# Turning a second softmax unit of five groups by VectorE and DMAs in a dense attention loop

## What is computed

```python
def latent_attention(q_nope, q_rope, k_nope, k_rope, v):
    ...
    def one_block(args):
        qn_b, qr_b = args
        s = (jnp.einsum('bqhd,bkhd->bhqk', qn_b, k_nope)
             + jnp.einsum('bqhr,bkr->bhqk', qr_b, k_rope)).astype(jnp.float32) * scale
        p = jax.nn.softmax(s, axis=-1).astype(v.dtype)
        return jnp.einsum('bhqk,bkhd->bqhd', p, v)
```

## Time and profile before

| | us |
|---|---|
| median of 3 runs | 606.72 (605.74 to 607.55) |
| profiled execution, its time | 606.28 |
| its span | 604.4 |
| TensorE busy | 595.3 (98%) |
| VectorE busy | 446.4 (74%) |
| ScalarE busy | 356.3 (59%) |
| GpSimd busy | 292.4 (48%) |
| hardware DMA queue, share of 16 engines | 56.2% |

### The profile page before, as it was taken

One profiled execution on the slowest core, in us unless ns is written; L12 is line 12 of the kernel. 1 busy time (PEld: TensorE's weight loads), 2 busy tenths in 40 slices (PEclk: granted clock), 3 DMA queues, 4 the chain that ended last, 5 costly groups with the idle time before them and its releaser, 6 DMA issues.

```text
span 604.4 us, 9197 instructions
## 1 busy us (share of the span) xinstructions
PE 595.3 (98%) x3076; PEld 484.0 (80%) x3076; DVE 446.4 (74%) x802; ACT 356.3 (59%) x762; POOL 292.4 (48%) x273
## 2 busy tenths in 40 slices
PE   8999999999999999999999999999999999999996
PEld 7888888788888888888887777777777777888885
DVE  5777663334434439898899788998998988799884
ACT  6644223213333228777787678788788788524563
POOL 4610702515656532536556537677677776510601
PEclk9999999999999999999999999999999999999998
DMA  7587457774776720101015967767768745598042
GB/s 246 190 287 203 155 166 242 230 259 149 245 262 226 224 69 1 36 1 36 2 27 114 242 157 185 190 179 191 192 172 199 203 127 182 177 386 326 1 173 107
DMA packets 72431, 102.11 MB, mean 169 GB/s; under 512 B 10232, under 2 KB 43008, under 8 KB 72384
## 3 DMA queue, kind: packets, MB, share of 16 engines
q1 hardware_dynamic: 72224, 101.25, 56.2%
q10 hardware_dynamic: 160, 0.27, 0.1%
HBM read 60.17 MB, written 31.62 MB: 152 GB/s over the span
## 4 chain that ended last, share of the span: by engine, by line
PE 78%; DMA 8%; DVE 5%; ACT 3%; POOL 2%; SPq 2%; issue 1%; ACTq 0%; DVEq 0%
PE ps L1824 13%; PE ps L1826 13%; PE ps L1825 13%; PE ps L2118 9%; PE ps L2096 7%; PE ps L2026 5%; PE ps L2031 5%; PE ps L1996 3%; PE ps L2046 2%; DMA lat_scratch<-lat_b 2%; PE ps L2006 2%; DMA lat<-lat_scratch 2%; PE ps L1983 2%; PE ps L1982 2%; PE ps L2007 2%; DMA ukv_raw<-w_ukv 1%
## 5 line engine op out<-in xcount | busy, mean ns | idle before, releaser
L1674 DVE TENSOR_TENSOR pT_lo<-ps,pT_hi 128x512 fp32r<-128x512 f32 x102 | 69.3, 684 | 21.5 <-ACT pT_hi L1237 20.3
L1824 PE MATMUL ps<-hT_hi,w_hi 128*128 128x512 f32 x208 | 84.0, 404 | 0.0
L1826 PE MATMUL ps<-hT_hi,w_lo 128*128 128x512 f32 x208 | 81.4, 391 | 0.0
L1825 PE MATMUL ps<-hT_lo,w_hi 128*128 128x512 f32 x208 | 81.1, 390 | 0.0
L1224 ACT ACTIVATE p_b<-ps,stat 128x1024 f32<-128x1024 f32 x64 | 71.3, 1114 | 12.6 <-DVE stat L1649 12.2
L1649 DVE TENSOR_REDUCE stat<-ps 128x1 f32<-128x1024 f32 x64 | 76.5, 1212 | 2.2 <-PE ps L2046 2.0
L1237 ACT ACTIVATE pT_hi<-ps 128x512 fp32r<-128x512 f32 x102 | 60.4, 596 | 23.8 <-PE ps L2096 23.5
L2096 PEld LDWEIGHTS ps<-ident,p_b 128*128 128x128 f32 x408 | 48.7, 140 | 17.4 <-issue 5.2
L2096 PE MATMUL ps<-ident,p_b 128*128 128x128 f32 x408 | 62.0, 275 | 0.6 <-DVE pT_lo L1674 0.3
L810 POOL TENSOR_SCALAR p_w<-p_w,stat 128x384 f32<-128x384 f32 (+1 forms) x40 | 24.4, 623 | 55.7 <-DVE stat L1557 55.7
L926 POOL TENSOR_TENSOR pT_lo<-p_land,pT_hi 128x512 fp32r<-128x512 f32 x26 | 33.3, 1286 | 29.5 <-ACT pT_hi L1244 29.5
(11 more groups left out here) (222 smaller groups left out, 1506.2 us busy)
## 6 DMA issues: line engine op xcount, KB each, us to landing
w_raw<-w_in SPq DMA_DIRECT2D x13, 512.0 KB, 4.5
probs_scratch<-p_blk SPq DMA_DIRECT2D x52, 128.0 KB, 2.8
p_land<-probs_scratch SPq DMA_DIRECT2D x13, 512.0 KB, 4.2
x_in<-x SPq DMA_DIRECT2D x8, 512.0 KB, 3.8
wt_raw<-w_out SPq DMA_DIRECT2D x8, 512.0 KB, 4.4
t_scratch<-wt_hi SPq DMA_DIRECT2D x16, 256.0 KB, 2.6
t_scratch<-wt_lo SPq DMA_DIRECT2D x16, 256.0 KB, 2.8
q<-q_h SPq DMA_DIRECT2D x16, 256.0 KB, 3.7
```

The costliest lines, as they stand in the source:

```text
L1674: nc.vector.tensor_tensor(pT_lo[at_], ps[:, 4 + a, :].rearrange("p (k c) -> p k c", c=P), f(pT_hi[at_]), ALU.subtract).then_inc(s_bTl, 1)
L1824: nc.tensor.matmul(o, a_hi, b_hi, start=first, stop=False, skip_group_check=goes_on)
L1825: nc.tensor.matmul(o, a_hi, b_lo, start=False, stop=False, skip_group_check=goes_on)
L1826: return nc.tensor.matmul(o, a_lo, b_hi, start=False, stop=last, skip_group_check=goes_on)
```

## The change

- A list `SECOND = [9, 21, 25, 37, 41]` joins the routed units: the second unit of the groups 2, 5, 6, 9 and 10. These five are no longer turned by TensorE, but by VectorE and DMAs. `FIRST` is the old list.
- VectorE turns a SECOND unit in pair U+1, between the two maxima of that pair. ScalarE copies its first half before the first exponential of pair U+5 and its second half after it. GpSimd subtracts both halves in one step. In `pv_b`, each part waits for the last routed unit of its group.
- `p_blk` and `p_land` are there twice, and each waits for the use two routed units earlier. The stores and fetches of the two parities count on semaphores of their own.
- SyncE stores a SECOND unit right behind the stores of the first unit, then fetches the first unit; the second fetch stands where the first stood.
- `v_raw` holds two pairs of heads instead of all eight heads, 8 KB a partition instead of 16; the second `p_blk` and `p_land` lie in the 8 KB that this leaves. Heads 1, then 2 and 3, are loaded ahead; heads 4 and 5 at the end of h = 3, heads 6 and 7 at the end of h = 5, with 512 KB each.

```diff
-        ROUTED = list(range(4, 56, 4))
+        FIRST = list(range(4, 56, 4))
+        SECOND = [9, 21, 25, 37, 41]
+        ROUTED = sorted(FIRST + SECOND)
...
             def store_probs(U):
                 i = ROUTED.index(U)
                 sp.wait_ge(s_pblk, NT + i + 1)
+                if i >= 2:
+                    sp.wait_ge(s_pin[i % 2], 16 * (NT // 2 + i // 2))
...
                 store_probs(U)
+                if U + 1 in SECOND:
+                    store_probs(U + 1)
+                    fetch_probs(U)
                 copy_k_rows(h)
                 fetch_recips(2 * h - 3)
-                fetch_probs(U)
+                fetch_probs(U + 1 if U + 1 in SECOND else U)
                 copy_q_c(h, s_dup)
                 store_recips(2 * h - 2)
                 store_probs(U + 4)
+                if U + 5 in SECOND:
+                    store_probs(U + 5)
+                    fetch_probs(U + 4)
                 if h + 1 < HEADS:
                     load_qk(h + 1)
-                fetch_probs(U + 4)
+                fetch_probs(U + 5 if U + 5 in SECOND else U + 4)
                 fetch_recips(2 * h - 2)
+                if h in (3, 5):
+                    i = h // 2 - 1
+                    sp.wait_ge(s_sp2, 2 * i + 2)
+                    sp.dma_start(v_raw[:, i, :, :], v_all[:, :, (4 + 2 * i) * HD:(6 + 2 * i) * HD]).then_inc(s_vr, 16)
...
-                if U - 6 in ROUTED:
+                if U - 6 in FIRST:
                     routed_hi(U - 6, 1)
+                if U - 5 in SECOND:
+                    routed_hi(U - 5, 0)
                 if U >= 2:
                     pT_b_hi(U - 2, 0)
                 exp_b(U)
+                if U - 5 in SECOND:
+                    routed_hi(U - 5, 1)
...
                 max_b(U)
+                if U - 1 in SECOND:
+                    turn_probs(U - 1)
                 if U >= 2:
                     pT_b_lo(U - 2, 0)
                 max_b(U + 1)
...
-                if 4 * G in ROUTED:
-                    n = 2 * ROUTED.index(4 * G) + part % 2 + 1
+                if group_routed(G):
+                    n = 2 * ROUTED.index(group_routed(G)[-1]) + part % 2 + 1
                     pe.wait_ge(s_phi, NT + n) if part < 2 else pe.wait_ge(s_plo, NT + n)
```

More of the change, by code:

```diff
@@ L181, in encoder @@
         o_b = at("o_b", 197, [P, 2, HALF])
-        p_blk = at("p_blk", 132.5, [P, 4, NT, Q32])
-        p_land = at("p_land", 136.5, [P, SEQ])
+        p_blk = [at(f"p_blk{i}", kb, [P, 4, NT, Q32]) for i, kb in enumerate((132.5, 105))]
+        p_land = [at(f"p_land{i}", kb, [P, SEQ]) for i, kb in enumerate((136.5, 109))]
         r_row = [at(f"r_row{c}", kb, [P, HALF]) for c, kb in enumerate((203, 146.5))]
@@ L233, in encoder @@
         s_xT, s_hhi, s_hT = sem("xT_done"), sem("hT_hi_ready"), sem("hT_ready")
-        s_xblk, s_xsto = sem("x_blocks_turned"), [sem(f"x_blocks_stored{i}") for i in range(2)]
+        s_xblk, s_xsto = sem("x_blocks_turned"), [sem("x_blocks_then_odd_probs_stored"), sem("x_blocks_stored1")]
         s_xq = [sem(f"x_turned_then_t_parts_in{i}") for i in range(4)]
@@ L956, in _ @@
             for U in range(B_UNITS + 8):
-                if U - 5 in ROUTED:
+                if U - 5 in FIRST:
                     routed_lo(U - 5, range(0, 1))
-                if U - 6 in ROUTED:
+                if U - 6 in FIRST:
                     routed_lo(U - 6, range(1, 2))
+                if U - 6 in SECOND:
+                    routed_lo(U - 6, range(2))
                 if U // NT + 1 < HEADS:
@@ L1234, in pT_b_hi @@
                     act.wait_ge(s_gh, 1) if U == 0 else act.wait_ge(s_g, 2 * NM)
-                if (U % 4 == 0 or U % 4 == 1 and U - 1 in ROUTED) and a == 0 and G >= 2:
+                if all(v in ROUTED for v in range(4 * G, U)) and a == 0 and G >= 2:
                     act.wait_ge(s_bpv, G - 1)
```

62 lines of the change are left out of this document (35 added, 27 removed).

## The result

| | before | after |
|---|---|---|
| median, same chip | 606.57 (605.74 to 607.55) | 632.2 (630.92 to 634.97) |
| profiled execution, its time | 606.28 | 630.92 |
| its span | 604.4 | 629.1 |

The change makes the kernel slower: the ratio is 1.043, interval 1.041 to 1.046. The forecast was 617.0 with a range up to 621, so the direction was right and the size was not: 25.6 us were lost where 10.3 were forecast.

A forecast was written before the change was run, and what follows sets the result against it. TensorE was taken to bound the stage, with little room elsewhere. Terms 1 and 2 (6.9 us) plus term 3 (3.4) gave 10.3 on 606.28, or 616.6; 0.44 for the median of runs made 617.0, range 603 to 621.

The forecast's parts named there:

- What bounds the kernel: Dense attention: TensorE bounds the stage; a second chain of scores, two maxima and exponential ends only 0.43 us before its matmuls.
- What is removed: TensorE loses two sets of four transposes per second unit: 0.88 us a unit, 4.4 us for five.
- The sign that I named: In the profile after, TensorE's busy time about 4.4 us smaller with a longer span.
- Term 1: Pairs 10, 22 and 38: VectorE's turn between the two maxima lengthens the chain to the rope matmuls, 1.4 us in all.
- Term 2: TensorE waits for ScalarE's copy of the second unit: 3.9 us in pairs 14, 30, 46; 1.6 in pairs 26, 42.
- Term 3: Late landings of units 25 and 41, lengthening pairs 30 and 46: 3.4 us, bounds 1.4 and 10.5.
- GpSimd nothing, V by pairs nothing: GpSimd's two more subtractions a unit and loading V by pairs of heads were each taken to cost nothing.
- landings in time: Rival: the queue has room, so only terms 1 and 2 stand: 613.6 us, chance 0.15.
- The saved transposes come through: Rival: TensorE's shorter stream in pairs 10, 22, 26, 38, 42 saves 0.88 us each: 602.3 us, half 604.5; chance 0.20.
- The queue pauses as before: Rival: late landings cost term 3's upper bound, 10.5 us: 624.1 us, chance 0.08.
- The two cancel: Rival: early ScalarE copies and small losses in pairs 10, 22, 38 offset gains elsewhere: 606.7 us within 0.3%, chance 0.09.

The follow-up runs named there:

- few bytes: Changed kernel, but second units' stores carry 8 of 256 columns and their fetch 8 of 1024, order and waits kept: 621.56 us, ratio 1.025.
- the new order: Changed kernel with SyncE's DMAs reordered: both stores and fetches before Q rows, next head's Q and K loads before second unit's stores: 619.95 us, ratio 1.023.
- the square: Four kernels, all or few bytes, in changed kernel's SyncE order or the new order; the last row, few bytes with the new order, measured 615.32 us.
- the first run: Changed kernel with no second units, keeping the doubled buffers and V loads by pairs: 606.16 us against 606.94, ratio 0.9994.

## Why the prediction was wrong, point by point

- **What bounds the kernel**: right as far as it went. Rope matmuls, maxima and exponential did have only some 0.4 us of slack. But a third chain, from turn over stores and fetch to ScalarE's copy, had no more at unit 36 and less than 1 us at five other units, and I looked at it last.
- **What is removed**: 0.88 us a unit forecast; 0.76 seen in pair 22 with the turn moved behind the maxima, 0.91 at best (pair 42 with units 9, 25 and 41). The sign that I named, TensorE's busy time about 4.4 us smaller, did not come: it was 4.1 larger, and with few bytes, the new order and the full clock 595.5 us, 0.2 larger than before.
- **Term 1**: forecast 1.4, measured 0.68 + 0.31 + 0.31 = 1.30. Right.
- **Term 2**: forecast 3.9 + 1.6, measured in the few-bytes kernels 1.23 + 1.21 + 1.24 = 3.7 and 0.75 + 0.79 = 1.5. Right.
- **Term 3**: forecast 3.4 with bounds 1.4 and 10.5; terms 1 and 2 come to 6.5, which leaves 24.8 - 6.5 = 18.3. This is the step that failed, in four ways. (Its upper bound has a slip, too: 421.4 and the pauses of before, 1.5 and 1.6 us, are 424.5 and not 425.2, so 3.8 us late and not 4.5. It changes nothing here.)
  - I summed the work of the queue and let the DMAs go out as soon as the engines were free. The step read "counting from 396.0" and named no wait of SyncE. The stores of unit 24, turned by 410.1, went out from 413.4 on, behind a split that waited for loads that stood behind unit 21's turn. With few bytes the square puts 4.3 and 4.2 us on this in pairs 30 and 46, with all bytes 1.8 and 4.7; in the whole kernel it is 6.6 or 11.6 us.
  - Unit 9 was put at 0 and units 21 and 37 weren't asked at all, since I took only stretches with another second unit ahead. A first and a second unit in a row are enough: pair 14 waited 0.85 us, pairs 26 and 42 lost up to 4.8 and 5.9.
  - The median fetch took 5.1 us (4.2 in before) where I used 4.1, and unit 25's took 7.3. In the whole kernel the second units' bytes are worth 10.4 us in after's order.
  - The clock: no row of before had a slice below 9 in the attention, and I counted a wait as its own length. Some 5.5 us of the 24.8 are work at a lower clock.
- **GpSimd nothing, V by pairs nothing**: the first run shows it for V when no second unit is there; with them, moving the V loads changed nothing that could be told from scatter, and no run leaves them out. (What leaves the start of the stage is heads 4 to 7, 1.0 MB and not 1.3.) For GpSimd's subtractions no run tests it; GpSimd was late in after, but by waiting for K.
- **The rivals**: "landings in time" (613.6) would have needed the last row of the square. It came to 615.3 with nearly no bytes. The Trainium skill (DMA: Bandwidth & Descriptors, Specifications) gives about 358 GB/s to HBM, by which the queue had room; the trace doesn't agree, as share 0.99 came at 264 GB/s here. "The saved transposes come through" was right for single pairs only, -0.76 in pair 22 with the late turn. "The queue pauses as before" (624.1), to which I gave 0.08, was the nearest, and still 8 us short: it let the queue pause, but not wait for a split. "The two cancel" came in no run with a second unit.

Where the saving went: five times some 0.7 to 0.9 us came off TensorE's stream, 1.3 + 5.2 were spent in the two waits of terms 1 and 2, over and above it, and the rest is late landings and the lower clock behind them. The detour replaces 0.71 us of TensorE's time by a chain of turn, four stores, a round trip and a fetch, two in a row, whose time could be hidden for one unit in four and not for two.

## What to carry to other kernels

Before giving work to a DMA detour, write down for each of its DMAs what stands ahead of it in the issuing queue and what that waits for, and not only how full the engines are. Compare the landing of the load with the start of its reader in the old kernel: where that slack is near zero, whatever delays the new transfers bring come out as gaps of the compute engines. Take a difference in one pair of one trace with care where a landing decides it: here a fetch scattered by 1.5 us and the pair by 2.8. And count a gap of some microseconds on TensorE at more than its length, if the profile shows the clock falling behind such gaps.
